# A decoder step with mixture of experts: the last stage's loads, scaling and norm chains rearranged

## The reference

```python
h2 = rmsnorm(x, g_ffn)
# every row picks one of 4 groups of experts by argmax, and the best 2 of its 8 experts
weight = p_g[:, None] * p_e            # two weights per row
# per expert (32 of them, width 256), for its rows:
a = silu(xb @ w1[e]) * (xb @ w3[e]);  out = (a @ w2[e]) * w
x = x + hier_moe(h2, ...)              # the two experts' rows are added
y = rmsnorm(x, g_final)                # y_prompt and y_sample
```

## Time and profile before

| | us |
|---|---|
| median of 3 runs | 1198.14 |
| span of the profiled execution (first to last instruction) | 1198.1 |
| to the first issue of expert weights | 747.7 |
| experts, to the last scatter issued | 383.9 |
| last scatter to the first load of results | 3.3 |
| first load to the end of the last VectorE instruction | 55.0 |
| from there to the end | 8.1 |

### The profile page before, as it was taken

How to read it: one execution, slowest core, us unless ns; L and a number is a source line. 1 busy time by engine, 2 the same in 40 slices (tenths; PEclk the granted TensorE clock), 3 DMA queues, 4 the chain that set the end, 5 groups by cost and what they waited for, 6 DMA issues and landing times. The chain is left out here.

```text
span 1198.1 us, 18619 instructions
## 1 busy us (share of the span) xinstructions
PE 1026.9 (86%) x5380; PEld 876.4 (73%) x5381; DVE 815.4 (68%) x2040; ACT 455.6 (38%) x904; POOL 220.5 (18%) x273
## 2 busy tenths in 40 slices
PE   4889999999999999999989999349999999999500
PEld 4888888888788887888868887237878787877400
DVE  6574566555565556755565443779999999999496
ACT  6221112111211113011122110238888888888332
POOL 0001220022100121012200000112333333332133
PEclk9899999999999999999989998569999999999855
DMA  9131015010330105101164211628999999998172
GB/s 317 36 97 50 19 49 165 10 50 10 116 100 10 49 15 173 38 22 41 31 243 155 92 54 38 279 76 321 360 360 364 366 367 368 363 363 313 51 317 105
DMA packets 73377, 190.25 MB, mean 159 GB/s; under 512 B 12449, under 2 KB 47357, under 8 KB 59845
## 3 DMA queue, kind: packets, MB, share of 16 engines
q1 hardware_dynamic: 61236, 163.90, 37.3%
q0 software_dynamic: 12064, 25.39, 5.8%
HBM read 171.67 MB, written 34.45 MB: 172 GB/s over the span
## 5 line engine op out<-in xcount | busy, mean ns | idle before, releaser
L996 DVE TENSOR_TENSOR w_lo<-w,w_hi 128x512 fp32r<-128x512 f32 x256 | 160.1, 686 | 4.4 <-ACT w_hi L673 4.2
L673 ACT ACTIVATE w_hi<-w 128x512 fp32r<-128x512 f32 x256 | 141.2, 630 | 6.7 <-PE bank L773 4.2
L771 PE MATMUL bank<-w_hi,xT_hi 128*128 128x512 f32 x256 | 104.8, 409 | 17.2 <-DVE xT_lo L1007 11.2
L1605 PE MATMUL bank<-wvg_hi,hT_hi 128*128 128x512 f32 x288 | 117.5, 408 | 0.3 <-DVE wvg_lo L1648 0.3
L1605 PE MATMUL bank<-wvg_lo,hT_hi 128*128 128x512 f32 x288 | 114.0, 396 | 0.0
L1605 PE MATMUL bank<-wvg_hi,hT_lo 128*128 128x512 f32 x288 | 113.5, 394 | 0.0
L1479 ACT ACTIVATE v<-bank 128x256 f32<-128x256 f32 x36 | 13.8, 382 | 251.7 <-PE bank L1606 251.7
L771 PE MATMUL bank<-hT_hi,wuqk_hi 128*128 128x344 f32 x288 | 98.0, 340 | 12.0 <-DVE qT L1782 6.7
L773 PE MATMUL bank<-w_hi,xT_lo 128*128 128x512 f32 x256 | 101.4, 396 | 0.0
L772 PE MATMUL bank<-w_lo,xT_hi 128*128 128x512 f32 x256 | 101.0, 395 | 0.0
L772 PE MATMUL bank<-hT_lo,wuqk_hi 128*128 128x344 f32 x288 | 95.2, 330 | 1.1 <-issue 1.1
(11 more groups left out here) (235 smaller groups left out, 2397.5 us busy)
## 6 DMA issues: line engine op xcount, KB each, us to landing
w<-in_w_dram SPq DMA_DIRECT2D x96, 1024.0 KB
raw<-in_w_in_dram SPq DMA_DIRECT2D x72, 256.0 KB, 3.2
parts<-part_d SPq DMA_DIRECT2D x8, 1024.0 KB, 10.5
xall<-in_x_prompt_dram SPq DMA_DIRECT2D x8, 512.0 KB, 8.1
mixed_d<-mixed POOLq DMA_DIRECT2D x32, 128.0 KB, 2.1
sample_state<-in_state_ret_dram SPq DMA_DIRECT2D x16, 256.0 KB, 3.7
out_dram<-sample_state SPq DMA_DIRECT2D x16, 256.0 KB, 3.9
mixed_in<-mixed_d SPq DMA_DIRECT2D x8, 512.0 KB, 4.8
```

The source lines that it names most:

```text
L673: act.activation(hi, whole_w, ACT.Copy).then_inc(S["up_hi"], 1)
L771: pe.matmul(out, lhs[0], rhs[0], start=first, stop=False)
L996: dve.tensor_tensor(lo, whole_w, hi, ALU.subtract).then_inc(S["up_lo"], 1)
L1605: g = pe.matmul(gates, x[xi], wvg[wi][:, 1:3, k, :], start=first, stop=last)
```

## The change

- `parts` gets 9 buffers, so no load of results waits for an add, and all 9 are issued at once. The `z` buffers are gone; `gfin_b` and a scratch tile move to another place, and `gfin_b` is loaded before the first expert weights.
- The result is formed in `x2` by one VectorE instruction a tile, x2 * (1/rms) * g_final (`scale_rows`). The last tile is done and stored in two halves of 512 columns. ScalarE and GpSimd multiply nothing any more.
- The chains for 1/rms run on GpSimd, in five groups of tiles, (0 to 2), (3, 4), (5, 6), (7), (8). ScalarE's square takes the factor 1/D. Each chain is still 15 instructions.
- VectorE's order is `TAIL`: add 0 to 4, scale 0 to 2, add 5 and 6, scale 3 and 4, add 7 and 8, scale 5 to 8.
- On GpSimd the spill test comes ahead of the wait for the three scatter semaphores.

The declarations of semaphores are left out, and empty lines:

```diff
--- before.py
+++ after.py
...
@@ -300,11 +300,9 @@
         rf = Region(nc, at_W, 2 * 3 * KT * (P + DV) * 4)
-        NPART, NZ = 5, 4
-        parts = [rf.place(f"parts{i}", [P, 2, D], F32) for i in range(NPART)]
-        zt = [rf.place(f"z{i}", [P, D], F32) for i in range(NZ)]
-        gfin_b = rf.place("gfin_b", [P, D], F32)
-        junk_f = rf.place("junk_f", [P, D], F32)
+        parts = [rf.place(f"parts{i}", [P, 2, D], F32) for i in range(NT)]
+        gfin_b = rc.place("gfin_b", [P, D], F32)
+        junk_f = rc.place("junk_f", [P, D], F32)
         SS, MS, RS = 0, 9, 18
         HX, TX = 27, 36
...
@@ -339,9 +337,9 @@
         w2_in = [sem(f"w2_in{i}") for i in range(SLOTS)]
         xg_in = [sem(f"xg_in{i}") for i in range(SLOTS)]
         part_out = [sem(f"part_out{i}") for i in range(SLOTS)]
-        part_in = [sem(f"part_in{i}") for i in range(NPART)]
+        part_in = [sem(f"part_in{i}") for i in range(NT)]
         gfin_in = sem("gfin_in")
-        y_out = [sem(f"y_out{i}") for i in range(NZ)]
+        y_out = sem("y_out")
         mix_out = [sem(f"mixed_out{i}") for i in range(2)]
         by_pe = {n: sem(n) for n in (
...
@@ -514,11 +511,15 @@
         def rows_of(n):
             return slice(0, NB if ORDER[n] == CH else P)
-        def y_stored_before(eng, n):
-            if n >= NZ:
-                eng.wait_ge(y_out[n % NZ], 16 * (n // NZ))
+        def halves_of(n):
+            return (slice(0, D),) if n < NT - 1 else (slice(0, 512), slice(512, D))
+        NORM_GROUPS = ((0, 3), (3, 5), (5, 7), (7, 8), (8, 9))
+        TAIL = [("add", n) for n in range(5)] + [("scale", n) for n in range(3)] + [("add", 5), ("add", 6)]             + [("scale", 3), ("scale", 4), ("add", 7), ("add", 8)] + [("scale", n) for n in range(5, 9)]
+        def group_of(n):
+            return [a <= n < b for a, b in NORM_GROUPS].index(True)
         def load_mixed(sp, t, s):
             if not is_first(t, 2):
...
@@ -590,6 +591,7 @@
                 down_weights(sp, b - 1, (s - 1) % SLOTS)
             sp.wait_ge(S["w_mm"], after(NT))
+            sp.dma_start(gfin_b[:, :], g_final.unsqueeze(0).to_broadcast([P, D])).then_inc(gfin_in, 16)
             blocks(sp, weights)
             sp.wait_ge(S["down_used"], after(4 * (NE - SLOTS)))
             down_weights(sp, NE - 1, (NE - 1) % SLOTS)
...
@@ -608,21 +610,15 @@
             sp.wait_ge(S["parts_ready"], after(1))
             for n, t in enumerate(ORDER):
                 r = rows_of(n)
-                sp.wait_ge(S["x3_done"], after(n - NPART + 1))
-                sp.dma_start(parts[n % NPART][r, :, :].rearrange("p j n -> p (j n)"),
+                sp.dma_start(parts[n][r, :, :].rearrange("p j n -> p (j n)"),
                              part_d[2 * t * P:2 * (t * P + r.stop), :].rearrange("(p j) n -> p (j n)", j=2))\
-                    .then_inc(part_in[n % NPART], 16)
-                if n == 2:
-                    sp.dma_start(gfin_b[:, :], g_final.unsqueeze(0).to_broadcast([P, D])).then_inc(gfin_in, 16)
+                    .then_inc(part_in[n], 16)
             for n, t in enumerate(ORDER):
                 dst = y_prompt[0, t * P:(t + 1) * P, :] if t < CH else y_sample.rearrange("b o d -> (b o) d")
-                if n < 7:
-                    sp.wait_ge(S["y_done"], after(n + 1))
-                else:
-                    sp.wait_ge(S["y2_done"], after(n - 6))
-                sp.dma_start(dst, zt[n % NZ][rows_of(n), :]).then_inc(y_out[n % NZ], 16)
-            for s in range(NZ):
-                sp.wait_ge(y_out[s], 16 * len(range(s, NT, NZ)))
+                for half in halves_of(n):
+                    sp.wait_ge(S["y_done"], after(n + 1 + half.start // 512))
+                    sp.dma_start(dst[:, half], x2[rows_of(n), t, half]).then_inc(y_out, 16)
+            sp.wait_ge(y_out, 16 * (NT + 1))
         def stage_c_act(act):
...
@@ -752,18 +748,12 @@
             spilled(act, more)
-            act.wait_ge(S["parts_ready"], after(1))
             for n in range(NT):
                 r = rows_of(n)
                 act.wait_ge(S["x3_done"], after(n + 1))
                 act.wait_ge(S["sq3_done"], after(n))
-                act.activation(junk_f[r, :], x2[r, ORDER[n], :], ACT.Square, accum_out=small[r, SS + n:SS + n + 1])\
-                    .then_inc(S["sq3_done"], 1)
-                for u in {3: (0, 1, 2), 6: (3, 4, 5), 8: (6,)}.get(n, ()):
-                    act.wait_ge(S["rstd3_done"], after(u // 3 + 1))
-                    y_stored_before(act, u)
-                    act.activation(zt[u % NZ][rows_of(u), :], x2[rows_of(u), ORDER[u], :], ACT.Identity,
-                                   scale=small[rows_of(u), RS + u:RS + u + 1]).then_inc(S["z_done"], 1)
+                act.activation(junk_f[r, :], x2[r, ORDER[n], :], ACT.Square, scale=D ** -0.5,
+                               accum_out=small[r, SS + n:SS + n + 1]).then_inc(S["sq3_done"], 1)
         def three(pe, out, lhs, rhs, first, last):
...
@@ -1052,38 +1042,30 @@
             spilled(dve, more)
-            dve.wait_ge(S["parts_ready"], after(1))
             many = Steps(dve, steps_f)
             def add_parts(n):
-                r, t, slot = rows_of(n), ORDER[n], n % NPART
-                dve.wait_ge(part_in[slot], 16 * (n // NPART + 1))
-                many.do(dve.scalar_tensor_tensor(out=x2[r, t, :], in0=parts[slot][r, 0, :], scalar=pair_w[r, t, 0:1],
+                r, t = rows_of(n), ORDER[n]
+                dve.wait_ge(part_in[n], 16)
+                many.do(dve.scalar_tensor_tensor(out=x2[r, t, :], in0=parts[n][r, 0, :], scalar=pair_w[r, t, 0:1],
                                                  in1=x2[r, t, :], op0=ALU.mult, op1=ALU.add))
-                dve.scalar_tensor_tensor(out=x2[r, t, :], in0=parts[slot][r, 1, :], scalar=pair_w[r, t, 1:2],
+                dve.scalar_tensor_tensor(out=x2[r, t, :], in0=parts[n][r, 1, :], scalar=pair_w[r, t, 1:2],
                                          in1=x2[r, t, :], op0=ALU.mult, op1=ALU.add).then_inc(S["x3_done"], 1)
-            def norms(i):
-                a, b = 3 * i, 3 * i + 3
-                dve.wait_ge(S["sq3_done"], after(b))
-                ms, rs = small[:, MS + a:MS + b], small[:, RS + a:RS + b]
-                many.do(dve.tensor_scalar(ms, small[:, SS + a:SS + b], 1.0 / D, EPS, ALU.mult, ALU.add))
-                many.do(rsqrt_guess(many, dve, ms, rs, bits[:, a:b]))
-                newton_rsqrt(many, dve, ms, rs, small[:, HX + a:HX + b], small[:, TX + a:TX + b])\
-                    .then_inc(S["rstd3_done"], 1)
-            for n in range(NT):
-                add_parts(n)
-                if n in (3, 6):
-                    norms(n // 3 - 1)
-            norms(2)
-            dve.wait_ge(S["rstd3_done"], after(3))
+            def scale_rows(n):
+                r, t = rows_of(n), ORDER[n]
+                for half in halves_of(n):
+                    dve.scalar_tensor_tensor(out=x2[r, t, half], in0=x2[r, t, half], scalar=small[r, RS + n:RS + n + 1],
+                                             in1=gfin_b[r, half], op0=ALU.mult, op1=ALU.mult)\
+                        .then_inc(S["y_done"], 1)
             dve.wait_ge(gfin_in, 16)
-            for n in (7, 8):
-                y_stored_before(dve, n)
-                dve.scalar_tensor_tensor(out=zt[n % NZ][:, :], in0=x2[:, ORDER[n], :], scalar=small[:, RS + n:RS + n + 1],
-                                         in1=gfin_b[:, :], op0=ALU.mult, op1=ALU.mult).then_inc(S["y2_done"], 1)
+            for kind, n in TAIL:
+                if kind == "add":
+                    add_parts(n)
+                else:
+                    dve.wait_ge(S["rstd3_done"], after(group_of(n) + 1))
+                    scale_rows(n)
         def route(dve, st):
...
@@ -1259,8 +1241,6 @@
             blocks(pool, step_m)
             for b in range(NE - SLOTS, NE):
                 scatter(b, b % SLOTS, MAIN_USES[b % SLOTS], b % 2)
-            for s in range(SLOTS):
-                pool.wait_ge(part_out[s], 16 * MAIN_USES[s])
             def more(b, i):
                 pool.wait_ge(S["xt2_mm"], after(2 * b))
...
@@ -1271,15 +1251,17 @@
                 carried(pool, "pool")
             spilled(pool, more)
+            for s in range(SLOTS):
+                pool.wait_ge(part_out[s], 16 * MAIN_USES[s])
             pool.sem_inc(S["parts_ready"], 1)
-            pool.wait_ge(gfin_in, 16)
-            for n in range(7):
-                r = rows_of(n)
-                pool.wait_ge(S["z_done"], after(n + 1))
-                pool.tensor_tensor(zt[n % NZ][r, :], zt[n % NZ][r, :], gfin_b[r, :], ALU.mult)\
-                    .then_inc(S["y_done"], 1)
+            for a, b in NORM_GROUPS:
+                ms, rs = small[:, MS + a:MS + b], small[:, RS + a:RS + b]
+                pool.wait_ge(S["sq3_done"], after(b))
+                carried(pool, "pool")
+                steps.do(pool.tensor_scalar(ms, small[:, SS + a:SS + b], EPS, None, ALU.add))
```

(13 more changed lines are left out.)

## The result

| | us |
|---|---|
| changed kernel, median of 20 runs | 1199.68 (1193.33 to 1205.44) |
| kernel before, median of 20 runs on the same chip | 1195.26 (1192.21 to 1199.7) |
| ratio after to before | 1.0034, 95% interval 1.0021 to 1.0047 |

The account below looks back on a forecast made before the run. VectorE, or what it waits for, was taken to set the end. Laid out in time, VectorE's halves end at 1192.7 against 1189.96 before; plus 6.4 gives 1199 us, 1 above before; range of 8 in 10: 1187 to 1206.

Parts of the forecast that it names:

- Spill test: On GpSimd, before the first load: testing ahead of the scatter waits makes everything 0.96 us earlier.
- Loads: VectorE's 1.88 us wait for tile 3 goes; issuing all loads at once brings no more.
- Scalings: All adds take 1.28 us again, saving 14.5 us; scalings add 8.3; VectorE's own work is 34 us.
- Norm chains: On GpSimd: one step per VectorE instruction while VectorE is busy, one in 0.39 us while it is idle.
- The five waits: VectorE waits for GpSimd's chains ahead of scalings: 4.3, 3.2, 3.5, 5.1 and 5.5 us.
- Rival B: Chains on GpSimd aren't held up by adds, 0.39 us a step throughout: 1186 us, faster by 1.0%; chance 0.18.
- Rival C: GpSimd makes no step while VectorE is busy; 20 steps fall into idle time: 1207 us, slower by 0.7%; chance 0.14.
- the copies in the earlier trace: Small GpSimd copies beside VectorE subtractions: each ended 0.03 to 0.05 us after the instruction in flight, leaving subtractions at 0.69.
- the other end: Alternative to no VectorE cost: each of 20 GpSimd steps holds VectorE 0.2 us, 4 us in all.
- The Trainium skill: Whichever of VectorE (two SBUF inputs) and GpSimd starts first holds the shared ports; by it VectorE would pay 4 us.
- The books: Totals for the change: 28 us saved; 30 us added, 8.3 of scalings and 21.6 of waiting for GpSimd.
- The end: After VectorE's last instruction: 1.9 us to the last packet, 4.5 us behind it, 6.4 in all instead of 8.14.

Follow-up runs that it names:

- e4: Changed kernel with the spill test put back behind the waits for the scatters; 1199.53 us, ratio 1.0029 to the kernel before.
- e7: Changed kernel with load n waiting until tile n-5 has been added, as before, nine buffers kept; 1200.57 us, ratio 1.0041 to the kernel before.
- e11: Changed kernel with the g_final load back behind the third load of parts and VectorE waiting for it ahead of each scaling; 1201.01 us, ratio 1.0040.
- e8: Kernel before with only the nine scalings moved to VectorE, one instruction each, chains on VectorE as before; 1185.9 us, ratio 0.9919.
- e10: Changed kernel with a VectorE wait ahead of each scaling and add 5 for the previous scaling's end, making gaps; ratio 1.0014 to the kernel before.
- e3: Changed kernel with each add of 1024 columns cut into two of 512; ratio 1.0013 to the kernel before.
- e1: Changed kernel with its five 1/rms chains on VectorE, each ahead of its first scaling; 1185.61 us, ratio 0.9919 to the kernel before.
- e2: Changed kernel with ten more small dependent GpSimd instructions behind its last chain, result unread; 1204.34 us, ratio 1.0072 to the kernel before.
- e5: Changed kernel with only the last of the five chains (tile 8) on VectorE; 1193.82 us, ratio 0.9984 to the kernel before.
- e6: Changed kernel with all chains on VectorE, only two of them, reordered so no square is waited for; 1178.93 us, ratio 0.9858.
- e9: Changed kernel with the 8-row tile's scaling behind those of tiles 1 and 2; ratio 1.0018 to the kernel before.

## Why the prediction was right, step by step

- *Spill test*: 0.96 us forecast, 1.06 measured (3.33 to 2.27; e4).
- *Loads*: the wait of 1.88 us ahead of tile 3 fell to 0.40, and issuing all at once brought nothing (e7). Of the 1.88 us booked as saved about 1.1 came through to the first scaling (e11).
- *Scalings*: all adds at 1.28 us, VectorE's work 33.9 us against 34. Alone this part is worth 10.7 us (e8), more than the 6.2 that the prediction's terms give (14.5 less 8.3), because it also lets GpSimd's program end early: 6.0 us came from VectorE's stretch and 4.9 from the end.
- *Norm chains*: one step per VectorE instruction beside it, 0.39 us a step otherwise. The five waits were forecast as 4.3, 3.2, 3.5, 5.1 and 5.5 us, and were 4.4, 4.3, 3.6, 5.1 and 5.5. The second is 1.1 too long by the step of 4.49 us (e10, without that step, had 3.1). Rival B is refuted by the timeline and by e3. Rival C, starvation, exists for three turns of 20, lost by one step that began to wait while an 8-row instruction was in flight. VectorE paid nothing for the small steps, as the copies in the earlier trace rows had it, and not the 4 us of the other end.
- *The Trainium skill*'s rule (SBUF — State Buffer, "SBUF: two separate sides") held in the direction in which VectorE comes first: GpSimd waited to the end of the 128-row instruction in flight. Beside the 8-row scaling one step did not: it began 0.05 us after it (1152.36 and 1152.31) and took 0.22 us. In the other direction, VectorE blocked for a whole GpSimd instruction, no run here shows it for steps of 0.2 us: adds stayed at 1.27 to 1.29 us with steps beside them, and in e11 the scalings at 1163.30 took 2.48 us, as in the changed kernel, though a step had begun 0.02 us ahead of them.
- *The books* of the prediction don't quite meet: 30 us added less 28 saved is 2, while the layout in time, by which the forecast goes, gives 2.7 (1192.7 against 1189.96).
- *The end* is the step that was mis-sized, and its reason was wrong. I read 4.5 us behind the last packet as fixed and took 6.4 us from VectorE's end; it was 7.75, and it is GpSimd's drain of 9.0 us that sets it (e1, e2, e5). With 1.35 us here, and 1.3 in the middle stretch (1.1 of it the long step), the tail grew by 3.6 us where 1.0 was forecast. These 2.6 us were small enough to leave the forecast, no change beyond half a per cent, standing. That the time itself, 1199.68, came so near to 1199 is in part luck: the forecast added its 1 us to an execution slower than the median, and from the median of 1195.26 it would have been 1196.3.

All in all the change joins a good part and a bad one. The scalings on VectorE alone bring 10.7 us; putting the chains on GpSimd costs 12.5 against the same kernel with them on VectorE (e1), through the waits and through the drain.

## What to carry to other kernels

A helper engine that is idle on average is not free when its steps wait their turn behind the main engine's: price a dependent chain on it at one step per instruction of the main engine where both use SBUF, and look at whether the main engine then waits for it. Before the end of a program is put down to stores, look at which engine's queue drains last: here, once the 9.0 us behind GpSimd's last instruction reached past the stores, later work on it pushed the end out by as much, so its last instruction belongs early. And in this kernel two short chains on the main engine, placed so that it never waits for a square (e6), beat every other arrangement tried here, all those with chains on GpSimd included.

## What the runs showed of the hardware that I had not expected

GpSimd's drain at the end of the program took 8.98 us in e1, e2, e6 and e8, whether it began 9 us or 55 us ahead of the end of the span, and ended 9.0 us after GpSimd's last instruction in before, changed and e5. VectorE's drain in the changed kernel, 1.45 us from 1190.8, ended 0.1 us after VectorE's last instruction. A GpSimd instruction that began to wait beside an 8-row VectorE instruction missed its turn there, and in the changed kernel also those at the ends of the two 128-row scalings that followed without a gap (4.49 us; 2.23 in e9, where an add with a gap behind it came next); one that began to wait beside a 128-row instruction got its turn at the end of it.
